# Mixture of experts: seven of eight experts take their tokens sorted into tiles of 128

## The reference

```python
def swiglu(h, wg, wu, wd):
    return (jax.nn.silu(h @ wg) * (h @ wu)) @ wd

def moe_swiglu(h, router, bias, wg, wu, wd):
    logits = (h @ router).astype(jnp.float32) + bias.astype(jnp.float32)
    top_logit, top_idx = lax.top_k(logits, TOP_K)          # TOP_K = 2
    top_w = jax.nn.softmax(top_logit, axis=-1)
    gates = jnp.sum(jax.nn.one_hot(top_idx, N_EXPERTS, dtype=jnp.float32) * top_w[..., None], axis=-2)
    out = jnp.zeros_like(h)
    for e in range(N_EXPERTS):                              # 8
        out = out + gates[..., e:e + 1] * swiglu(h, wg[e], wu[e], wd[e])
    return out
```

## Time and profile before

| | |
|---|---|
| Median of 3 runs | 3061.71 us (3058.63 to 3061.96) |
| Profiled execution, whole | 3064.98 us |
| Its span, first to last instruction | 3063.2 us |
| PE busy | 2800.4 us, 91% |
| DVE busy | 2054.9 us, 67% |
| ACT busy | 1276.5 us, 42% |
| POOL busy | 4.5 us |
| Moved by DMA | 434.16 MB, mean 142 GB/s |

### The profile page before, as it was taken

How to read it: one execution, slowest core, us unless ns; L and a number is a source line. 1 busy time by engine, 2 the same in 40 slices (tenths; PEclk the granted TensorE clock), 3 DMA queues, 4 the chain that set the end, 5 groups by cost and what they waited for, 6 DMA issues and landing times.

```text
span 3063.2 us, 59451 instructions
## 1 busy us (share of the span) xinstructions
PE 2800.4 (91%) x24380; PEld 2695.4 (88%) x24380; DVE 2054.9 (67%) x3649; ACT 1276.5 (42%) x1980; POOL 4.5 (0%) x10
## 2 busy tenths in 40 slices
PE   7989899998988998899789998897888999999999
PEld 7878899897888998798679997787887999999999
DVE  5888667488876757674557767655565666666665
ACT  4444444344434444333334434232443444444443
POOL 0000000000000000000000000000000000000000
PEclk9999999999999999898899998897998999999999
DMA  5443445454443553221225553111422555555554
GB/s 194 160 136 123 160 155 183 144 181 151 138 145 132 192 175 111 84 71 69 81 100 176 178 179 106 51 67 49 151 96 92 199 184 182 179 177 193 182 186 159
DMA packets 143052, 434.16 MB, mean 142 GB/s; under 512 B 15776, under 2 KB 26272, under 8 KB 142528
## 3 DMA queue, kind: packets, MB, share of 16 engines
q1 hardware_dynamic: 138688, 424.68, 41.5%
q10 hardware_dynamic: 4096, 5.67, 0.6%
HBM read 429.25 MB, written 1.05 MB: 140 GB/s over the span
## 4 chain that ended last, share of the span: by engine, by line
PE 73%; DVE 17%; ACT 5%; issue 4%; DMA 0%; DVEq 0%; ACTq 0%
PE ps L1592 21%; PE ps L1594 20%; PE ps L1593 20%; PE ps L1597 10%; DVE wl L2283 4%; DVE b L2287 3%; DVE b L2295 3%; ACT wh L1986 2%; DVE SC L2295 2%; DVE SC L2287 1%; DVE RS L2287 1%; ACT SC L2065 1%; ACT b L1996 1%; DVE SC L2291 0%; PE ps L1600 0%
## 5 line engine op out<-in xcount | busy, mean ns | idle before, releaser
L1592 PE MATMUL ps<-b,wh 128*128 128x256 f32 x3712 | 1075.7, 290 | 109.6 <-DVE wl L2283 67.2
L2283 DVE TENSOR_TENSOR wl<-wf,wh 128x1024 fp32r<-128x1024 f32 (+2 forms) x850 | 959.5, 1163 | 273.1 <-ACT wh L1986 271.5
L1594 PE MATMUL ps<-b,wl 128*128 128x256 f32 x3712 | 1063.1, 286 | 0.0
L1593 PE MATMUL ps<-b,wh 128*128 128x256 f32 x3712 | 1061.1, 286 | 0.0
L1986 ACT ACTIVATE wh<-wf 128x1024 fp32r<-128x1024 f32 (+2 forms) x850 | 822.5, 1004 | 360.8 <-PE ps L1594 300.0
L1592 PEld LDWEIGHTS ps<-b,wh 128*128 128x128 f32 x3712 | 725.0, 195 | 123.7 <-issue 88.2
L1592 PE MATMUL ps<-HH,wh 128*128 128x256 f32 x2496 | 721.4, 289 | 12.9 <-DVE wl L2283 12.8
L1593 PEld LDWEIGHTS ps<-b,wh 128*128 128x128 f32 x3712 | 725.0, 195 | 0.2
L1594 PEld LDWEIGHTS ps<-b,wl 128*128 128x128 f32 x3712 | 724.0, 195 | 0.0
L1593 PE MATMUL ps<-HL,wh 128*128 128x256 f32 x2496 | 711.3, 285 | 0.0
L1594 PE MATMUL ps<-HH,wl 128*128 128x256 f32 x2496 | 710.8, 285 | 0.0
(11 more groups left out here) (188 smaller groups left out, 1830.8 us busy)
## 6 DMA issues: line engine op xcount, KB each, us to landing
wf<-in_w_in_b SPq DMA_DIRECT2D x112, 512.0 KB, 4.1
wf<-in_moe_wg SPq DMA_DIRECT2D x88, 512.0 KB, 3.3
wf<-in_moe_wu SPq DMA_DIRECT2D x88, 512.0 KB, 4.4
wf<-in_w_in SPq DMA_DIRECT2D x80, 512.0 KB, 4.1
wf<-in_moe_wd SPq DMA_DIRECT2D x64, 384.0 KB, 3.1
wf<-in_w_ffn_g SPq DMA_DIRECT2D x44, 512.0 KB, 3.2
wf<-in_w_ffn_u SPq DMA_DIRECT2D x44, 512.0 KB, 4.3
wf<-in_moe_wd SPq DMA_DIRECT2D x64, 320.0 KB, 3.4
```

Source lines behind the costliest of these rows:

```text
L1592: e.matmul(o, stat[0], mov[0], start=first, stop=False)
L1593: e.matmul(o, stat[0], mov[1], start=False, stop=False)
L1594: return e.matmul(o, stat[1], mov[0], start=False, stop=end)
L2283: e.tensor_tensor(u.wlo, u.buf, u.whi.bitcast(F32), SUB).then_inc(u.lo[0])
```

## The change

Expert 0 stays as it was, with its gate row. Experts 1 to 7 are computed in tiles of 128 token places. After routing, `h` is turned so that tokens lie on partitions (`xt_turn`, eight steps of four matmuls), and a product with a triangular matrix gives each token its rank in each expert's list (`ranks`). For each tile, DVE makes a selection matrix `SEL` of ones and zeros from ranks and mask (`choose`), PE turns it and sums the gates (`pick`), and PE gathers the tile's tokens by 32 matmuls with `SEL` (`gather`). In the tile's products the tokens are stationary and the weights move, 512 columns at a time (384 in the third part of the up-projection). Three parts of gate and value, each with four units, make `FF`. Eleven transposes turn it (`tile_turn`). The down-projection is eleven units of two matmul groups of 512 columns (`tile_down`), and 16 matmuls put the 128 results back to their tokens (`scatter`), from where DVE adds them to `X`.

A tile is 24 + 11 = 35 units: 27 of 1024 columns, 8 of 768. Its products are 162 matmuls of 512 moving columns and 48 of 384, in place of 792 of 256 for an expert.

There are ten tiles: one for each of the seven experts, and three more for experts that have more than 128 tokens. Which experts these are is known only on the chip: DVE works out row numbers (`over`, `over_tokens`), and POOL fetches the three tiles' 105 units row by row with an index (`indirect_dma_start`), where SP skips them. The three tiles run in every execution, with an empty selection where no expert has too many. The host lays out the experts' weights in the order of the units.

```diff
+            if t.rows is None:
+                return unit_of(ins[name][t.e8 - 1, at].rearrange("(b p) n -> p b n", b=1), 1, n)
+            return unit_of(ins[name].rearrange("e u p n -> (e u p) n"), 1, n, t.rows[i])
...
+        for i, t in enumerate(tiles):
+            p = past(i - 1)
+            up_half(t, 0, 0)
+            if p:
+                turn_up(p, 2)
+            up_half(t, 0, 1)
+            if p:
+                down_tile(p)
+            else:
+                yield from gemm("add_x0", pairs(ins["moe_wd_2"], 0, 8), 11, kcols(F0), fd0, to_x)
+                tiles[0].f0 = list(end0)
+            turn_up(t, 0)
+            up_half(t, 1, 0)
+            if p:
+                for n in range(4):
+                    scatter(p, n)
+            next(more, None)
+            if i + 1 < len(tiles):
+                choose(i + 1)
+            up_half(t, 1, 1)
+            if i + 1 < len(tiles):
+                pick(i + 1)
+            up_half(t, 2, 0)
+            turn_up(t, 1)
+            if i + 1 < len(tiles):
+                gather(i + 1)
+            up_half(t, 2, 1)
...
+        def gather(st):
+            E.wait_ge(st.t.sel, st.xt)
+            E.wait_ge(st.bk.free)
+            for i in range(4):
+                k = 4 * st.c + i
+                for b in range(2):
+                    r = mm(st.bk.ps[:, i * 128:(i + 1) * 128], st.XT[st.z][:, b, k * 128:(k + 1) * 128], st.t.SEL[:, b, :], b == 0, b == 1)
...
+        def tile_up(st):
+            E.wait_ge(st.t.xg)
+            E.wait_ge(st.bk.free)
+            for p in st.pieces:
+                E.wait_ge(p.u.hi)
+                E.wait_ge(p.u.lo)
+                for k in range(p.k0, p.k1):
+                    c = slice((k - p.k0) * st.w, (k - p.k0 + 1) * st.w)
+                    r = product(st.bk.ps[:, 0:st.w], [x[:, k, :] for x in st.t.XG], (p.u.whi[:, c], p.u.wlo[:, c]), k == 0, k == 7)
+                r.then_inc(p.mark[0])
...
+        for u in units:
+            if u.rows is not None:
+                E.wait_ge(units[u.i - NRAW].hi)
+                E.wait_ge(units[u.i - NRAW].lo)
+                E.wait_ge(u.rows[1])
+                e.indirect_dma_start(u.buf, None, u.src, bass.IndirectOffsetOnAxis(ap=u.rows[0], axis=0)).then_inc(u.raw[0], 16)
...
+            if u.rows is not None:
+                continue
```

More of the change, by code:

```diff
@@ L1531, in routing @@
[L1531 to L1570, removed]
+            gts, idr = st.done, st.idr
+            for b in range(2):
+                for z in range(2):
+                    for c in range(2):
+                        st = step("xt_turn")
+                        st.b, st.z, st.c, st.bk, st.rdy, st.XT, st.IDR = b, z, c, a_bank(), [hall, idr], XT, IDR
+                        xt.append(emptied(st.bk))
+                    yield
@@ new lines, in routing @@
+            st = step("ranks")
+            st.bk, st.MASK, st.RK, st.TRI, st.rdy = a_bank(), MASK, RK, TRI, [gts, t_r]
+            rk = emptied(st.bk)
+            dg = step("gate_diag")
+            dg.DG, dg.GT, dg.rdy, dg.done = DGm, GT, gts, P.next("gate_diag")
+            for e8 in range(1, 8):
+                tiles.append(tile(e8, [MASK[:, b, e8:e8 + 1] for b in range(2)], [RK[:, 8 * b + e8:8 * b + e8 + 1] for b in range(2)],
+                                  [GT[:, b, e8:e8 + 1] for b in range(2)], [rk, gts]))
@@ new lines, in pick, with gather @@
+        def pick(i):
+            t, p = tiles[i], past(i - 2)
+            st = step("pick")
+            st.t, st.IDR, st.bk = t, IDR, a_bank()
+            st.war = [p.scattered, p.f_done] if p else None
+            t.sides, t.seen = emptied(st.bk), st.bk.full
+        def gather(i):
+            t, p = tiles[i], past(i - 2)
+            t.xg = []
+            for c in range(2):
+                for z in range(2):
+                    st = step("gather")
+                    st.t, st.c, st.z, st.XT, st.xt, st.bk = t, c, z, XT, xt, a_bank()
+                    st.war = p.up_done if p else None
+                    t.xg.append(emptied(st.bk))
+                    t.gathered = st.bk.full
@@ new lines, in scatter, with to_x @@
+        def scatter(t, n):
+            st = step("scatter")
+            st.t, st.n, st.DD, st.bk = t, n, DD, bank(Gb)
+            st.bk.at, st.bk.full = st.bk.i, P.next("scattered")
+            st.x, st.fac, st.plain, st.before = row(x3[:, 2 * n:2 * n + 2, :]), 1.0, True, x_ready[n]
+            x_ready[n] = emptied(st.bk)
+            t.scattered = st.bk.full
+        fd0 = yield from first_up(ins["moe_wg_2"], ins["moe_wu_2"], 11, F0, ADDED, routing)
+        end0 = []
+        def to_x(n, st):
+            st.x, st.before = row(x3[:, 2 * n:2 * n + 2, :]), [x_ready[n], hall]
+            emptied(st.bk)
+            st.gate, st.sc, st.gb = GB[:, 0, :], Scr.take(), gb
+            st.done = st.sc.out = x_ready[n] = P.next("x0")
+            end0[:] = [st.bk.full]
@@ L1572, in build @@
+        turn_up(t, 2)
+        down_tile(t)
+        for n in range(4):
+            scatter(t, n)
     t_vec = P.next("ld_vec", 16)
@@ new lines, in xt_turn, with ranks, choose @@
+        def xt_turn(st):
+            if st.z == 1:
+                E.wait_ge(st.bk.full)
+                e.tensor_copy(st.XT[1][:, st.b, st.c * 512:(st.c + 1) * 512], st.bk.ps[:, :]).then_inc(st.bk.out[0])
+        def ranks(st):
+            E.wait_ge(st.bk.full)
+            e.tensor_copy(st.RK, st.bk.ps[:, 0:24]).then_inc(st.bk.out[0])
+        def choose(st):
+            t = st.t
+            E.wait_ge(t.rdy, st.war)
+            for b in range(2):
+                ins = ts(t.SEL[:, b, :], st.IOTA, t.rank[b], t.mask[b], ALU.is_equal, MUL)
+            ins.then_inc(st.done[0])
@@ L2904, in dve_program @@
+        table = dict(xt_turn=xt_turn, ranks=ranks, choose=choose, gather=gather, tile_gate=tile_gate, tile_value=tile_value, tile_turn=tile_turn,
+                     tile_down=tile_down, scatter=add_x_step, over=over, over_tokens=over_tokens,
+                     split=split_step, x_low=x_low, scaled_rsb=scaled_rsb, copy_rs=copy_rs, copy_rs_w=copy_rs, shift_rs=shift_rs, shift_rs_w=shift_rs,
                      up_gate=up_gate, up_gate_w=up_gate, up_rs=up_rs,
```

290 lines of the change are left out of this document (268 added, 22 removed).

## The result

The changed kernel takes 3071.24 us (median of 20 executions, 3063.19 to 3080.52), the kernel before 3061.57 (20, 3057.43 to 3066.46): 1.0032 of it, 95% interval 1.0024 to 1.0040. The forecast was 3031 us and faster. The profiled execution took 3072.45 us, span 3070.6; the sum in the prediction gave 3034 and 3032.

The account below looks back on a forecast made before the run. PE was taken to bound the kernel, then the ring of four raw buffers: 3063.2 - 663 + 420 + 216 - 15 + 8 + 3 = 3032 us of span, forecast 3031 us, 8 in 10 within 2940 to 3108.

Parts of the forecast that it names:

- seven plain tiles: Tiles of experts 1 to 7 fed by SP: 60 us each (54 to 66), 420 us in all (378 to 462).
- three index tiles and `over_tokens`: Last three tiles, fetched by POOL: 72 us each, 216 in all (180 to 306); `over_tokens` 4.2 us on DVE.
- routing: Beside expert 0's up-projection: seven gate-row rounds go, new steps come, 15 us saved (nothing to 25).
- `over`, tail, all else: Tiny DVE operations of `over` and `over_tokens` add 8 us; copies, low parts and scatters at the end add 3.
- The landing in the ring's turn: Plain tiles, ring of four raw buffers: landing 3.85 us, middle of 3.3 and 4.4, in a turn of 6.4 us.
- The six us charged for DVE's other work: Plain tiles: half of DVE's 11.9 us of other work added to the ring's 54 us, giving 60.
- The matmuls of 512 columns: Tile products on PE: 0.226 us for each matmul of 512 moving columns, 162 of them a tile.
- The engines bind: Rival for all ten tiles: landing stays 3.3 us, transfers hide, 54 us a tile, whole 2935; chance 0.22 (2935 to 3000).
- The index fetch starves PE: Rival for the last three tiles: at 9.2 us landing they take 306 us, whole 3121; chance 0.18 (over 3068).
- The clock falls: Rival for the index tiles: PE at the half clock level needs 95 us a tile, adding 69, whole 3100; chance 0.06.
- DVE shuts POOL out: Rival: each index fetch waits one low part, tile 83 us, whole 3063; 0.09 shared with plain tiles at 64 to 65.
- The signs of being wrong: Plain tile at 54 or 66 us, index tile under 65 or over 80, or gather matmuls 0.2 us apart.

Follow-up runs that it names:

- the kernel with seven tiles: The changed kernel without its three extra index tiles, the seven sorted tiles alone: 2835.60 us, 0.9262 of the kernel before.
- POOL's plain transfers: The changed kernel with the three extra tiles' weights (those of experts 1 to 3) fetched by POOL without an index: 3049.32 us, 0.9956 of the kernel before.
- eight buffers: The changed kernel with four more raw buffers for the units after the first up-projection: 2967.55 us, 0.9696 of the kernel before.
- both changes: The changed kernel with eight raw buffers and ACT and DVE splitting three units ahead in place of two: 2952.72 us, 0.9650 of the kernel before.
- the kernel fed by SP: The changed kernel with the three extra tiles' weights fetched by SP with plain transfers in place of POOL's by index: 3034.45 us, 0.9913 of the kernel before.
- the look-ahead of three: The changed kernel, four raw buffers, with ACT and DVE splitting three units ahead in place of two in the tiles: 3073.26 us, 1.0031 of the kernel before.
- half fetches: The changed kernel with SP fetching only half of each unit's columns in the seven plain tiles: 3020.99 us, 0.9859 of the kernel before.
- half low parts: The changed kernel with DVE making low parts for half of the columns only in the seven plain tiles: 3049.69 us, 0.9949 of the kernel before.

## Why the prediction was wrong, point by point

The sum against what the traces and the kernels without parts show, in us of span:

| term | predicted | measured | from |
|---|---|---|---|
| seven experts out | -663 | -663 | 94.7 each |
| seven plain tiles | 420 | 443 | 63.3 each, five periods of the kernel with seven tiles |
| three index tiles and `over_tokens` | 220 | 235.6 | the kernel without them |
| routing | -15 | -12.0 | 55.4 (2311.44 to 2366.8) to 43.4 (2307.16 to 2350.6) |
| `over`, tail, all else | 7 | 3.8 | what is left to 7.4 |
| sum | -31 | +7.4 | 3063.2 to 3070.6 |

From -31 to +7.4 are 38 us: 23 of them are the plain tiles, 16 the index tiles with `over_tokens`, 3 the routing, less 3 of the rest.

*The landing in the ring's turn* is the step that failed: the mechanism, a ring of four that binds, was right, and this term of it was too small. The earlier trace rows had 3.3 us for a transfer far from the one before it and 4.4 for a close one, and the prediction took the middle. But a ring that binds issues each transfer as soon as a buffer is free, with the others in flight: all are close. The upper row was the one that answers to the case. With the measured 4.6 and 4.0 (in the kernel with seven tiles; 3.9 in the page above), a unit is 7.15 / 4 = 1.79, a small one 6.07 / 4 = 1.52, and a tile 27 x 1.79 + 8 x 1.52 = 60.5 in place of 54. The six us charged for DVE's other work were then 2.8 (63.3 - 60.5). Two errors in opposite directions: +6.5 and -3.2, 3.3 us a tile, 23 in all. That the plain tile came out at 63.3, near the 60 forecast, is in part luck: by the landing alone it would have missed by twice as much.

*The index tiles* have about the turn that was predicted: 8.5 stood there, and the trace has 8.7. The parts were others. The prediction had put all of it into a landing of 5.9 us, taken from SP's first transfers; in the trace 1.1 us pass before the fetch starts and 5.2 from there to ACT's read, so that the sum agrees is luck. The tiles take 227 us, 76 each, and not 72; 8.7 / 4 x 35 gives 76. The prediction had let DVE's other work vanish in the gaps; that it costs some 3 us here as in the plain tiles fits the number and was not tried by itself.

The Trainium skill, page "DMA: Bandwidth & Descriptors", section "Latency and other measured facts", would have put the difference to SP at 0.4 us a turn. For POOL's plain transfers these runs agree: 0.6 by the medians (14.9 / 3 / 35 x 4), 0.45 by the mean turns. By index it is 1.4.

*`over_tokens`* costs 2.8 us a tile by the windows above (66.1 against 63.3), 8 in all, where 1.4 a tile was charged; those tiles have seven DVE instructions more. It is no fixed price: with eight buffers such a tile is 57.9 against 56.6, with both changes 55.1 against 54.5, and in the kernel fed by SP, where single plain tiles differ by up to 2.3 us, no difference stands out (64.8 against 64.4).

*Routing* held: 12 us against 15, with the 32 gather matmuls of 128 columns in 3.69 us, 0.115 each, where the choice was 0.12:

```profile
2337.13 3.69 PE L1767 MATMUL ps<-b,b 128*128 128x128 f32 x32
```

Its clock did not stay at 1 as forecast, but at 0.88 in the window above, where it was 0.79.

*The matmuls of 512 columns* held (starts at 2436.39, 2436.62 and 2436.85, 0.23 apart), PE's 53 us a tile nearly: it is what is left when the ring is long enough, 54.5.

*The rivals.* "The engines bind" (54 us a tile, 2935) was priced right as a state: two more changes, buffers and look-ahead, reach it at 2952.7. It needed the 3.3 us landing or more buffers, and had neither. "The index fetch starves PE" needed 82 us a tile; at 76 it is a part of the loss, 37 us. "The clock falls" came in part. The first index window stood at 0.89 and took 1.8 us more than the second at 1.00, though only 25 of its fetches went by index against 36. In the second window nearly all fetches go by index, and with four buffers it takes 75.2 us at 1.00, 74.8 at 1.00 with the look-ahead of three, 76.4 at 0.98 with half fetches in the plain tiles and 78.8 at 0.95 with half low parts in them. So some us of an index tile go with the clock; whether the clock makes the tile longer or the gaps of a longer tile lower the clock, no run decides. With plain transfers from POOL both windows stood at 1.00. "DVE shuts POOL out" is real and adds 19 us of POOL's time in all, below.

*Chance and range.* Break-even was a plain tile 4.4 us slower than forecast (31 / 7), with 54 to 66 as the bounds and the likelier price at the upper one. 0.24 for slower was too little for a margin of 1% that hung on one middle between two rows. The signs of being wrong that the prediction named were wider than its margin: a plain tile at 63.3 (wrong from 66), an index tile at 76 (wrong over 80) and gather matmuls 0.115 apart trip none of them, and together they turn the forecast gain into a loss.

## What to carry to other kernels

When a change makes the consumer faster, work out the ring's turn (issue, landing, each reader, handovers) over its number of buffers, with the landing of a loaded queue, not the mean of what the relaxed kernel shows. If that comes near the new consumer's need, add buffers together with the change (at five the ring asked 27 x 1.55 + 8 x 1.27 = 52 us and still cost 1.7 over the 56.6 of eight): here 4 to 8 turned 0.3% slower into 3.0% faster, and a look-ahead of three, worth nothing by itself, made it 3.5%. Waits in the kernel before (ACT's 20.7 us for DMA) are the first sign of it, though there a deeper ring gained nothing; and fetches that POOL issues lengthen the turn, so they need the deeper ring most: with eight buffers nearly all of their price was gone.

## What the runs showed of the hardware

**A fetch by index that starts during a low part on DVE, which reads two SBUF operands, ends 0.82 us after it; a plain one from POOL doesn't wait.** POOL and DVE in the changed kernel, same stretch:

```profile
2859.76 0.94 POOL L3298 DMA_INDIRECT wf<-in_moe_up_a,b  x1 [0.30 <-DVE wl L2564]
2861.01 1.82 POOL L3298 DMA_INDIRECT wf<-in_moe_up_b,b  x1 [0.30 <-ACT wh L2233]
...
2860.78 1.23 DVE L2564 TENSOR_TENSOR wl<-wf,wh 128x1024 fp32r<-128x1024 f32 x1 [1.01 <-ACT wh L2233]
```

The second fetch starts while a low part runs, which ends at 2862.01; the fetch ends at 2862.83, 0.82 us behind it. Of the 105 fetches 51 started while a low part ran; they took 1.31 us in the mean, and 44 of them ended within 0.1 us of the low part's end plus 0.82. Three that started within 0.04 us of the low part's own start took 0.94, so these did not wait. The other 54 took 0.94, none over 0.97. In the kernel with both changes it is 64 of 75. With plain transfers from POOL 58 started in a low part, and none took more than 0.67. The Trainium skill, page "SBUF — State Buffer", section "Who interferes with whom", says that a DVE instruction with two SBUF inputs contends with GpSimd's reads and not with its writes. The trace agrees if the fetch by index reads its indices from SBUF, which no run here shows by itself; the prediction had used only the part on writing descriptors, which for `tensor_tensor` the page calls inferred, and so excused it. The price here is small, 51 x 0.37 = 19 us of POOL's time in three tiles; how much of it the tiles feel was not measured. It is read from the times of start and end, and no run was made to take the low parts out of POOL's way.

**A landing depends on what is in flight:** 512 KB took 3.3 us for the first of a pair in the kernel before, 4.6 in a ring of four at 274 GB/s, 5.3 in one of eight at 304 GB/s; 256 KB in the ring of four took 2.8. So a ring's gain from more buffers is less than its number says: from four to five the turn grew by about 0.6 us.

Open: what lowers the granted clock in some index tiles and what that costs alone, and why a fetch from POOL starts 0.5 us (plain) or 1.0 us (by index) later after the low part than one from SP.
